# One core, a hybrid decoder layer: order of weight splits, of the last pair's quarters and of DeltaNet slots, and two squares on another engine

## What is computed

```python
def gated_delta_rule(q, k, v, beta, g):
...
    def step(state, inp):
        u_i, w_i, qd_i, qk_i, kt_i, gl_i = inp
        v_new = u_i - jnp.einsum('bhcd,bhde->bhce', w_i, state)
        o = jnp.einsum('bhcd,bhde->bhce', qd_i, state) + jnp.einsum('bhcj,bhje->bhce', qk_i, v_new)
        state = state * jnp.exp(gl_i)[..., None, None] + jnp.einsum('bhcd,bhce->bhde', kt_i, v_new)
        return state, o
...
        dq = l2_normalize(dq.reshape(bsz, s, DN_HEADS, DN_HEAD_DIM))
        dk_ = l2_normalize(dk_.reshape(bsz, s, DN_HEADS, DN_HEAD_DIM))
...
        x = x + rms_norm(mixed, norm_g[l, 1])
        h = rms_norm(x, norm_g[l, 2])
        f = jnp.square(jax.nn.relu(h @ w_ff1[l])) @ w_ff2[l]
        x = x + rms_norm(f, norm_g[l, 3])
```

## Time and profile before

| what | us |
|---|---|
| median of 3 runs | 1894.82 (1894.42 to 1895.88) |
| the profiled execution | 1896.26 |
| its span | 1894.4 |
| TensorE busy in it | 1872.1 (99%) |
| VectorE busy | 1119.9 (59%) |
| ScalarE busy | 865.0 (46%) |
| GpSimd busy | 83.1 (4%) |

### The profile page before, as it was taken

How to read it: one execution, slowest core, us unless ns; L and a number is a source line. 1 busy time by engine, 2 the same in 40 slices (tenths; PEclk the granted TensorE clock), 3 DMA queues, 4 the chain that set the end, 5 groups by cost and what they waited for, 6 DMA issues and landing times.

```text
span 1894.4 us, 25282 instructions
## 1 busy us (share of the span) xinstructions
PE 1872.1 (99%) x9542; PEld 1516.9 (80%) x9542; DVE 1119.9 (59%) x1619; ACT 865.0 (46%) x1401; POOL 83.1 (4%) x63
## 2 busy tenths in 40 slices
PE   9999999999999999999999999999999999999998
PEld 7887777777887878888788788877888887888786
DVE  6714565674545354442445655568787876666767
ACT  7324555565344353533334334556434345434452
POOL 0000000000212212031000000000000000000000
PEclk9999999999999999999999999999999999999999
DMA  5322222223131131121534444545365667777867
GB/s 190 111 100 101 73 84 74 89 106 123 67 119 70 45 128 62 67 89 68 193 110 170 139 139 139 172 155 168 117 221 173 222 222 233 242 268 245 275 212 253
DMA packets 113351, 276.45 MB, mean 146 GB/s; under 512 B 12432, under 2 KB 12496, under 8 KB 113232
## 3 DMA queue, kind: packets, MB, share of 16 engines
q1 hardware_dynamic: 110928, 270.66, 41.9%
q10 hardware_dynamic: 2304, 4.20, 0.6%
HBM read 196.14 MB, written 78.68 MB: 145 GB/s over the span
## 4 chain that ended last, share of the span: by engine, by line
PE 87%; DVE 5%; DMA 3%; ACT 2%; issue 2%; SPq 0%; DVEq 0%; ACTq 0%
PE gemm L378 11%; PE gemm L380 11%; PE gemm L379 11%; PE dn L1802 2%; PE gemm L758 2%; PE dn L1804 2%; PE gemm L760 2%; PE gemm L759 2%; PE z L1701 2%; PE z L1933 2%; PE z L1937 2%; PE z L1936 2%; PE gemm L1890 2%; PE dn L1723 2%; PE gemm L1892 2%; PE gemm L1891 2%
## 5 line engine op out<-in xcount | busy, mean ns | idle before, releaser
L378 PE MATMUL gemm<-act_hi,w_hi 128*128 128x512 f32 x832 | 351.8, 423 | 0.5 <-issue 0.5
L380 PE MATMUL gemm<-act_hi,w_lo 128*128 128x512 f32 x832 | 326.8, 393 | 0.0
L379 PE MATMUL gemm<-act_lo,w_hi 128*128 128x512 f32 x832 | 325.6, 391 | 0.0
L356 DVE TENSOR_TENSOR w_lo<-w_raw,w_hi 128x1024 fp32r<-128x1024 f32 x114 | 143.1, 1255 | 203.2 <-ACT w_hi L352 178.6
L380 PEld LDWEIGHTS gemm<-act_hi,w_lo 128*128 128x128 f32 x832 | 156.7, 188 | 34.8
L378 PEld LDWEIGHTS gemm<-act_hi,w_hi 128*128 128x128 f32 x832 | 157.5, 189 | 30.9 <-issue 6.7
L379 PEld LDWEIGHTS gemm<-act_lo,w_hi 128*128 128x128 f32 x832 | 157.8, 190 | 27.9 <-issue 3.4
L424 ACT ACTIVATE stage<-gemm,cols 128x512 f32<-128x512 f32 x104 | 71.7, 689 | 237.5 <-PE gemm L380 233.4
L2121 DVE TENSOR_TENSOR_SCAN a_P<-a_keep,a_P,a_floor 128x512 f32<-128x512 f32 (+3 forms) x96 | 94.0, 1008 | 37.7 <-ACT a_keep L1217 37.3
L352 ACT ACTIVATE w_hi<-w_raw 128x1024 fp32r<-128x1024 f32 x102 | 107.2, 1051 | 18.7 <-PE gemm L1892 12.5
L2267 DVE TENSOR_TENSOR d_TT<-d_TT,dn 128x512 f32<-128x512 f32 x48 | 33.1, 689 | 134.6 <-PE dn L1804 134.6
(11 more groups left out here) (463 smaller groups left out, 4198.0 us busy)
## 6 DMA issues: line engine op xcount, KB each, us to landing
w_raw<-w_stream SPq DMA_DIRECT2D x142, 512.0 KB, 4.3
projections<-stage SPq DMA_DIRECT2D x60, 512.0 KB, 2.9
w_raw<-w_stream SPq DMA_DIRECT2D x112, 256.0 KB, 4.2
hidden_quarters<-mixed SPq DMA_DIRECT2D x92, 256.0 KB, 4.1
sum_x<-hidden_quarters SPq DMA_DIRECT2D x50, 256.0 KB, 4.0
gate<-projections SPq DMA_DIRECT2D x48, 256.0 KB, 2.7
f_t<-hidden_quarters SPq DMA_DIRECT2D x44, 256.0 KB, 4.5
d_in<-projections SPq DMA_DIRECT2D x12, 512.0 KB, 6.9
```

The costliest lines, as they stand in the source:

```text
L356: nc.vector.tensor_tensor(w_lo[s][:], w_raw[s][:].rearrange("p (k c) -> p k c", k=KT), w_hi[s][:].bitcast(f32), ALU.subtract).then_inc(lo_ ...
L378: nc.tensor.matmul(g_bank[hf][:], w_hi[s][:, k, :], a_hi[:, k, t], start=(k == 0), stop=False)
L379: nc.tensor.matmul(g_bank[hf][:], w_hi[s][:, k, :], a_lo[:, k, t], start=False, stop=False)
L380: last = nc.tensor.matmul(g_bank[hf][:], w_lo[s][:, k, :], a_hi[:, k, t], start=False, stop=(k == KT - 1))
```

## The change

Four edits:

1. In the first pass of the feed-forward part, ScalarE splits the weights first and takes the x1 tiles behind them, except in the last block, where the tile stays first.
2. In the last pair a quarter is split at more places: 6 behind (11,5), 7 to 9 behind (11,7), 10 and 11 behind (11,4), 12 and 13 in chunk 0, 14 and 15 in chunk 1. SP loads quarters 4 to 13 accordingly: two at each of products 2, 6, 5, 7, and 12 and 13 at product 4.
3. The DeltaNet slots' weights ahead of head 0 are 11, 2, 6 and were 11, 5, 7; a head's last slot is 5 and was 4.
4. For head 0, VectorE multiplies d_x0 and d_x1 by themselves in place of ScalarE's squares; the wait for the two stores of y moves there, ahead of the second.

```diff
-        DN_PRO = [11, 5, 7]
-        DN_HEAD = [2, 3, 1, 2, 1, 2, 1, 5] + [0, 2.72] * (NDS - 5) + [0, 1.5] + [1.2] * (2 * NCH) + [4]
+        DN_PRO = [11, 2, 6]
+        DN_HEAD = [2, 3, 1, 2, 1, 2, 1, 5] + [0, 2.72] * (NDS - 5) + [0, 1.5] + [1.2] * (2 * NCH) + [5]
...
-        FRONT = {(N_ST - 2, 3): [0, 1], (N_ST - 1, 2): [2, 3], (N_ST - 1, 6): [4, 5], (N_ST - 1, 7): [6, 7], (N_ST - 1, 4): [8, 9, 10]}
-        PREP = {0: [11, 12], 1: [13, 14, 15]}
+        FRONT = {(N_ST - 2, 3): [0, 1], (N_ST - 1, 2): [2, 3], (N_ST - 1, 6): [4, 5], (N_ST - 1, 5): [6], (N_ST - 1, 7): [7, 8, 9], (N_ST - 1, 4): [10, 11]}
+        PREP = {0: [12, 13], 1: [14, 15]}
...
-                if m == N_ST - 1 and p in (2, 6, 7):
+                if m == N_ST - 1 and p in (2, 6, 5, 7):
                     for u in range(2):
-                        load_quarter(4 + 2 * (2, 6, 7).index(p) + u)
+                        load_quarter(4 + 2 * (2, 6, 5, 7).index(p) + u)
...
                 if (m, p) == (N_ST - 1, 4):
-                    for u in (10, 11):
+                    for u in (12, 13):
                         load_quarter(u)
-            last_quarter, last_raw = 11, 3
+            last_quarter, last_raw = 15, 3
...
-                if (h, j) == (0, 1):
-                    for T in range(2):
-                        act.wait_ge(y_stored[T], 1 + 16 * 4)
-                if j < 2:
+                if j < 2 and h:
...
-                        for k in TILES_FF1[b][:1]:
+                        for k in TILES_FF1[b] if b == KT - 1 else ():
                             take_x1(1, k)
                     if n + 1 < PAIR_ST:
                         split_hi(act, n + 1, s)
...
-                        for k in TILES_FF1[b][1:]:
+                        for k in TILES_FF1[b] if b < KT - 1 else ():
                             take_x1(1, k)
                         square_hidden(b)
...
+            for j in range(2):
+                dve.wait_ge(dn_silu, j + 1)
+                if j:
+                    for T in range(2):
+                        dve.wait_ge(y_stored[T], 1 + 16 * 4)
+                nc.vector.tensor_tensor(d_r[j][:], d_x[j][:], d_x[j][:], ALU.mult).then_inc(dn_sq, 1)
```

More of the change, by code:

```diff
@@ L1100, in _ @@
                     last_quarter += 1
-                    if last_quarter not in (14, 15):
-                        load_quarter(last_quarter)
+                    load_quarter(last_quarter)
                 if 9 <= c < 17 and c % 2 == 0:
```

## The result

The changed kernel takes 1882.91 us in the median of 4 runs (1881.74 to 1883.87), the kernel before 1895.32 in 4, so 12.4 us less. The ratio on record is 0.9941 (95%: 0.9929 to 0.9953); it is not the quotient of these two medians, which is 0.9935.

The account below looks back on a forecast made before the run. TensorE, busy 1872.1 of 1894.4 us, was taken as the bound, so only its waits and slow clock could pay. Terms -3.4 - 2.6 - 1.7 - 0.7 = -8.4 gave a 1886.4 us median, range 1884.7 to 1892.0.

Parts of the forecast that it names:

- First half, -3.4: First feed-forward half: cutting the 6.02 us ScalarE-VectorE ring removes TensorE's w_lo waits, -3.4 us (bounds -2.5 and -3.4).
- Last pair, -2.6 and -1.7: Last pair: earlier load of quarters 12 and 13 removes the stall, -2.6 us; clock then stays full, -1.7 us.
- The margin: Last pair: load expected 3.0 us earlier against a TensorE wait of 2.60, leaving 0.4 us to spare.
- DeltaNet, -0.7: DeltaNet slots and squares: sum of the moved splits, waits and prologue, -0.7 us (bounds -2.0 and +1.9).
- item (5): DeltaNet: d_vn's existing wait of 1.3 us stays, since nothing in the change reaches it.
- d_wt: DeltaNet: the split ahead of head 1's two d_wt roots moves behind them, removing their 0.8 us wait.
- d_qk: DeltaNet: w_lo moves from ahead of both qk evictions to between them, -0.8 of a 1.1 us wait.
- The new d_vn wait in head 0: DeltaNet, head 0's scan: a w_lo lands just ahead of the d_vn copy, +1.05 us (bounds 0 and 1.2).
- Two more splits: DeltaNet: two weight splits land in another scan and at a head's end, +0.2 us.
- Prologue: DeltaNet prologue: four fewer steps before the first gram, squares moved to VectorE, -0.3 us (bounds -0.6 and +0.5).
- rival C: DeltaNet: twelve splits standing ahead of scan or level work make the kernel slower, 1899.7 us; chance 0.05.
- Rivals A, B and D: A: pair stays late, 0.18; B: two to four more DeltaNet splits delay, 0.14; D: neither stall goes, about 1894, 0.06.

Follow-up runs that it names:

- e3: Kernel before with only the new DeltaNet slot weights, squares left on ScalarE: 1896.13 us, ratio 1.0007.
- e4: Kernel before with only head 0's two squares moved to VectorE: 1895.11 us, ratio 0.9996.
- e5: Kernel before, with SP waiting for head 2's rows of decay to land before issuing the next store: 1892.33 us, ratio 0.9989.
- e2: Kernel before with only the last pair's quarter order and loads changed: 1891.97 us, ratio 0.9985.
- e8: Kernel before with the DeltaNet slots and the squares changed together, other parts as before: 1892.09 us, ratio 0.9984.
- e1: Kernel before with only the first feed-forward half's order changed: 1889.93 us, ratio 0.9979.
- e7: Changed kernel with head 1's scaled key taken in the eighth chunk of head 0's scan, not the sixth: 1883.20 us, 0.9942 against before.
- e9: Changed kernel with the scaled key later and SP's store held until head 2's rows of decay land: 1884.60 us, ratio 0.9946.
- e12: Changed kernel itself, unchanged, measured a third time: 1885.20 us.
- e10: Changed kernel itself, unchanged, measured a second time: 1884.67 us, ratio 0.9951.

## Why the prediction was wrong

**First half, -3.4: right in mechanism, a little small.** -3.81 in every run that has the edit, and so below the bound of -3.4 under which the prediction saw nothing. The 5.45 us per block and the uncoupled ring came out (5.44). Two errors in the sum nearly cancelled. Of the 0.9 us for the smaller waits, 0.37 stands at 1219.91, ahead of this stage, and is the 0.4 that is left above; only 0.24 and 0.28 lay in it. Against that, each stall here cost more than its idle time: from start to start the three are 2.53, 0.40 and 0.44 us longer than steady work, and the matmul behind each started another 0.11 late. That makes 3.7.

**Last pair, -2.6 and -1.7: right in size.** In the matched traces 2.55 us are the stall and 1.6 the half rate. The margin was not 0.4 us but next to nothing: VectorE splits the last two quarters from 1564.69 to 1565.98, and TensorE starts the chunk at 1566.12. Quarter 6 cost nothing, as forecast; the wait for the copied product is 0.8 us as before.
The ground for the clock was too simple. "I expect it to stay full once the stall is gone" came true, yet the stall does not bring the fall by itself. The first half's wait of 2.4 us was followed by 0.50 in e3, e4 and e5 and not in before, e2 and e8; the pair's wait of 2.4 to 3.0 us in before and e8 and not in e1, e3, e4 and e5. Stretches of e4, the two waits and what followed each:

```profile
1273.00:1275.60 2.60, 1.44 (x7) 0.86 (x5) 0.94 (x3) 2.30 (x4) 0.00 (x0) 1.00 0.86 178
1276.60:1280.00 3.40, 3.20 (x8) 2.53 (x9) 3.28 (x6) 0.68 (x2) 0.00 (x0) 0.50 0.90 282
1574.00:1577.00 3.00, 1.65 (x7) 1.42 (x8) 2.50 (x4) 1.71 (x4) 0.00 (x0) 1.00 0.89 301
1577.00:1582.00 5.00, 5.00 (x23) 4.13 (x23) 2.46 (x5) 3.61 (x7) 0.00 (x0) 1.00 0.44 139
```

The same kernel shows the fall behind the first wait and not behind the second, the reverse of the earlier trace rows. So 5 of these 12 waits of 2.4 to 3.0 us were followed by a fall, at about 1.6 us each, and it may come with either wait. Falls also came behind waits of 1.8 us (e1, e8) and not behind one of 2.0 (e5). The kernels without both waits (changed, e7, e9 to e12) show none between 150 and 1870. The Trainium skill (TensorE: Matmul & The Clock Gate, "HAM oscillation — how this bites in real kernels"), which the prediction cites, has it that a wait for data lets the clock drop: 5 of the 12 waits agree, 7 do not. What decides is open.

**DeltaNet, -0.7: the step that failed.** Measured -3.57 in the first profile, -2.22 and -2.85 in the others, all below the term's bound of -2.0 (its own terms at their lowest add up to -2.3; the range would still have ended above the first measurement). Two things were wrong: item (5), which left d_vn's wait in head 1 as it was, and the sizes of the other terms, which alone make -2.2 in e10, where that wait stayed whole. Term by term, from start to start of the matmuls in the changed kernel's trace:
- d_wt: 0.8 forecast, 1.0 gone.
- d_qk: "I take off 0.8"; nearly all of it went, 1.26 less 0.14 that is left. w_lo between the two evictions delays the second alone, and TensorE hardly waits for that.
- Waits of 0.2 us in other places of the trace before, which I left out for want of a row: three (at 481.27, 526.18 and 713.15), 0.2 to 0.3 each, gone.
- The new d_vn wait in head 0: +1.05 forecast, +1.0 measured, by the mechanism named. e7 confirms it.
- Two more splits, +0.2 forecast: behind head 0 the changed kernel's trace has no delay above 0.15 us that the trace of before does not have.
- Prologue: -0.3 forecast, -0.2 to the end of the second sum of squares. The wait of 0.3 us in front of that sum is gone, and the first sum starts 0.2 later, since VectorE's first square ends later than ScalarE's did. VectorE took 2.36 us for the two.
- "d_vn's wait of 1.3 us stays: nothing in the change reaches it." It went in the first profile, stayed whole in e10 (1.2) and half in e12 (0.6). The change does reach it: the projection block's end falls into a later slot behind the rows, and so the store of a projection is issued 3.57 us behind the row in place of 0.53. I looked at the engines' instructions that were moved and not at the transfers behind the row on SP's queue.

SP's issues in time, the second row and the store behind it, before:

```profile
665.58 0.43 SPq L862 DMA_DIRECT2D d_bB<-decay_beta_rows  x1
666.11 0.38 SPq L433 DMA_DIRECT2D projections<-stage  x1
```

After:

```profile
661.27 0.43 SPq L862 DMA_DIRECT2D d_bB<-decay_beta_rows  x1
664.84 0.34 SPq L433 DMA_DIRECT2D projections<-stage  x1
```

Splits out of step (rival C) did not happen: one split in one place, not twelve. Rivals A, B and D did not come either.

**The sum.** By the parts that repeat, 2.2 to 3.6 and 3.8 and 2.6 of stall are 8.6 to 10.0 us, with up to 1.6 from the clock; ratios of 0.9941 to 0.9951 are 9.3 to 11.2 us. Part of the miss was luck: the first profile of before was one with a fall of the clock and the changed kernel's one with a fast row, and measured again the kernel stood at the low end of the range. The DeltaNet term was too small in every one of the three.

## What to carry to other kernels

When an instruction is moved on one engine, follow also the stores and loads that its result sets free, and what they share the DMA engines with: a latency that looked fixed (6.5 us for the row) may be what it is because of its neighbours. Two edits that look independent can be one: test each alone before crediting either, as with the slots (+1.27, of which about 1.6 is a fall of the clock), the squares (-0.08) and both (-3.51). Where a wait hangs on a landing or on the clock, one profile shows a draw and not a constant, so measure the part in several.

## What was not expected of the hardware

One 512 KB load that stands at the same place in the program took 4.8 to 6.8 us, and 5.2 to 6.4 in the same kernel; with the new slots it was late in those profiles where one 16 KB instruction packet started ahead of its last part. The clock's fall to half followed 5 of 12 waits of nearly the same length; near 131 us, behind the same instructions, the half-rate stretch was 6.83 us long in five of fourteen profiles and 3.41 in the rest.
